# Two attentions: one softmax head at a time and outputs turned at the end, or four heads together and outputs that come out turned

## The chip, the cores and the metric

One core of one Trainium2 chip runs the whole kernel. The metric is the device time of one execution in microseconds; the figure given for a kernel is the median of several runs. The kernel before takes 1696.51 us (median of 3 runs, 1694.89 to 1697.32).

Engines in this text: PE (TensorE) multiplies matrices and also turns (transposes) tiles, DVE (VectorE), ACT (ScalarE) and POOL (GpSimd) work elementwise, SP issues most of the DMAs. Each engine works through its own instructions in order and waits on semaphores for the others.

## The reference, cut to what matters

A decoder trunk of two layers over 512 tokens of width 1024, float32. Each layer adds an attention mixer and then a mixture of experts (MoE) to `x`.

```
even layer: h = rms_norm(x); x += concat(mamba2(h), dsa(h)) @ even_w_out
   dsa: 8 heads of 64, one K and V shared by all heads; for each query the
        128 best earlier keys by an indexer score (selm masks out the others)
        p = softmax(q k^T / 8 + rel_bias);  out = p v
odd layer:  h = rms_norm(x); x += nsa(h) @ odd_w_out
   nsa: 8 heads of 128 in 2 groups of 4; each group has its own K and V for
        three branches: compressed blocks (31 keys), selected blocks, window
        out = g0 * softmax_c(..) v_c + g1 * softmax_s(..) v_s + g2 * softmax_w(..) v_w
each layer: x += MoE(rms_norm(x))    32 experts of 6 MB of weights, top 2 for each token
```

At 512 tokens the selected and the window branch both see all earlier keys, so their scores are as wide as the causal part of the row.

## The kernel before, in words

The layers run one after another: even mixer, MoE, odd mixer, MoE. The part that the change touches are the two softmax attentions, which share one class, `Attention` (line 348), and the head of the output projection that follows each of them, `outproj_pe` (545).

**Work of one attention.** Queries are cut into four tiles of 128 rows, taken from the last tile (i = 3, 512 visible keys) to the first (i = 0, 128 keys); `TILES` is (3, 2, 1, 0). The unit is one head and one branch of one tile, with L = 128 (i + 1) keys, or 31 in the compressed branch. The even attention has 32 units (8 heads, four tiles), the odd one 96 (8 heads, three branches, four tiles; per head: compressed, selected, window). A unit goes through:

1. scores, PE (411): q as stationary, keys as moving, into one of four score banks; in the even layer two heads go as a pair, each on 64 rows of the array, and for i > 0 a second matmul (417) adds the mask.
2. DVE (502): bias is added, the row minimum of the negated scores is taken, the result goes to `p` in SBUF (semaphore `lg`).
3. ACT (489): exp, with the row sum as a by-product (`ex`).
4. PE (428): p is turned in blocks of 128 keys into one of two banks (`tr`).
5. ACT or DVE (476): the turned p is copied to `pT` in SBUF (`copied_act`, `copied_dve`).
6. PE (446), the value products: pT stationary (128 keys by 128 queries), V moving (64 or 128 columns), one matmul for each block of 128 keys (`pv`). The output lies with queries on partitions. It is not normalized yet.

Per head (even: per pair of heads) POOL raises the sums to the power -1 and, in the odd layer, multiplies them by the gates (1314; 1655, 1657, 1659; `coef`). DVE then scales the output and, in the odd layer, adds the three branches (1318; 1663 to 1665; `o`). When four heads of a tile are finished, their scaled outputs are turned on PE (435) and copied to `mixT`, the stationary operand of the output projection (558). In the even layer the Mamba half of the rows is turned in the same way; it is ready before the attention starts.

**Order.** Everything is written out by hand in steps t. At step t PE does the scores of unit t, turns unit t-2 and multiplies unit t-3 by its values; DVE and ACT have matching loops. `p` has 4 slots, `pT` 2.

**After the attention.** `outproj_pe` waits for the DVE's part of the last unit, projects the first half of tile 3, turns what is left (`tail_turns`), and projects on. SP waits for the last `o` (`att.done`, 1956) and then issues the weights of the first two experts; those of the third wait until the projection has been added (`_add`, 1959).

Of the kernel before, what the change touches and what calls it, by code (L numbers as in the profile page):

```python
# [196 lines left out]
def build(nc, ins, out):  # L197
    ctx = ExitStack()
    with ctx:
# [24 lines left out]
        minus1 = sb("minus1", [P, 3])  # L224
# [123 lines left out]
        class Attention:  # L348
            def __init__(self, tag, order, branches, turns, work, weigh, finish, before=None):
                self.weigh, self.finish, self.order = weigh, finish, order  # L350
                self.NB = len(branches(*order[0]))

                self.seq, self.tail = list(turns.get(-1, [])), turns["tail"]
                for m, (i, j) in enumerate(order):
                    for b, br in enumerate(branches(i, j)):
                        self.seq.append(dict(br, m=m, b=b, i=i, j=j))
                    self.seq += turns.get(m, [])
                self.all = self.seq + self.tail

                self.base = dict.fromkeys(("a", "n", "act", "dve", "m"), 0) if before is None else before.after  # L360
                c = dict(self.base)
                for u in self.all:
                    u["n"] = c["n"]; c["n"] += 1
                    if "m" in u:
                        u["a"] = c["a"]; c["a"] += 1
                    c[u["copy"]] += 1
                    u["copied"] = c[u["copy"]]
                c["m"] += len(order)
                self.after = c
                self.by_n = {u["n"]: u for u in self.all}  # L370
                self.by_a = {u["a"]: u for u in self.all if "m" in u}
                self.p = at(work, 4, SEQ)
                self.pT = at(work + 4 * SEQ, 2, 4, P)
                self.negm = sb(f"{tag}_negm", [P, 4])
                self.sums = sb(f"{tag}_sums", [P, 4, self.NB])
                self.coef = sb(f"{tag}_coef", [P, 4, self.NB])
# [4 lines left out]
            def tiles(self, u):  # L381
                return [(kt, min(P, u["L"] - kt * P)) for kt in range((u["L"] + P - 1) // P)]

            def copied(self, eng, u):

                eng.wait_ge(self.sem(f"copied_{u['copy']}"), u["copied"])

            def finished(self, eng, m):

                if m >= 0:  # L390
                    eng.wait_ge(self.sem("o"), self.base["m"] + m + 1)
# [6 lines left out]
            def done(self, eng):  # L398
                self.finished(eng, len(self.order) - 1)

            def mixed(self, eng, i):

                for u in self.all:
                    if "src" in u and u["tile"] == i:
                        self.copied(eng, u)

            def scores(self, pe, us):

                for u in us:
                    self.scored(pe, u["a"] - 4)  # L410
                    mm = nc.tensor.matmul(score_bank[u["a"] % 4][:, 0:u["L"]], u["q"], u["k"],  # L411
# [3 lines left out]
                for u in us:  # L415
                    if "mask" in u:
                        nc.tensor.matmul(score_bank[u["a"] % 4][:, 0:u["L"]], identb[:], u["mask"],
                                         start=False, stop=True).then_inc(self.sem("qk"), 1)

            def turn(self, pe, u):  # L420

                if u["n"] - 2 in self.by_n:
                    self.copied(pe, self.by_n[u["n"] - 2])
                b = bank[2 + u["n"] % 2]
                if "m" in u:
                    pe.wait_ge(self.sem("ex"), u["a"] + 1)
                    for kt, w in self.tiles(u):
# [1895 lines left out]
```

## Time and profile before

| | |
|---|---|
| median of 3 runs | 1696.51 us |
| profiled execution | 1696.19 us, span 1694.4 us |
| even attention | 203.1 to 253.9 us of the span |
| odd attention | 1000.8 to 1122.3 us |
| PE busy over the span | 94% |

The profile is of one execution. Times in its rows are from the start of the span. In a row of the timeline the columns are start, length, engine, line, operation, what it writes and reads, shape, count. A matmul of 32-bit data shows as two instructions (two passes). The lengths of PE's rows contain a modelled tail that overlaps the next instruction, so what an instruction costs PE is read from start to start.

### The profile page before, as it was taken

To read this page: it belongs to the slowest core of one execution; us is meant where nothing else is said; L and a number is where in the kernel's file an instruction comes from. 1 tells how busy PE (TensorE), PEld (TensorE's weight loads), DVE (VectorE), ACT (ScalarE), POOL (GpSimd) and SP (SyncE) were. 2 spreads that over 40 slices of the span, in tenths; PEclk is the share of its full clock that TensorE was granted. 3 is DMA by queue.
4 is the path that set the end of the run, shared out by engine and by line. 5 is a ranking of instruction groups with operands and counts; after the bars stand their busy time and mean duration, and the time that the engine had idled before them with its cause. 6 is when DMAs were issued, how large, how long until landed. Compare 5 with 4: busy or idle time off the path is not lost.

```text
span 1694.4 us, 20980 instructions
## 1 busy us (share of the span) xinstructions
PE 1589.3 (94%) x7948; PEld 753.0 (44%) x7948; DVE 434.3 (26%) x1112; ACT 393.7 (23%) x897; POOL 200.4 (12%) x297
## 2 busy tenths in 40 slices
PE   7999899799999999998799989999799999999993
PEld 4545574433333333332446457855333333333331
DVE  1585651610000000000321235643500000000002
ACT  2444451311111111111100136632211111111110
POOL 1241220000000000000101012320000000000000
PEclk9999999899999999999899989999799999999997
DMA  7120307379999999999924120042699999999996
GB/s 236 64 86 7 112 5 297 137 300 421 421 422 421 422 421 423 422 422 371 302 34 170 39 66 2 1 184 115 250 413 422 421 421 422 422 422 422 423 422 248
DMA packets 117162, 467.24 MB, mean 276 GB/s; under 512 B 40346, under 2 KB 46746, under 8 KB 68205
## 3 DMA queue, kind: packets, MB, share of 16 engines
q1 hardware_dynamic: 107724, 449.63, 66.1%
q10 hardware_dynamic: 4256, 8.40, 1.4%
q0 software_dynamic: 5120, 8.41, 1.3%
q8 instruction: 36, 0.59, 0.1%
q14 instruction: 26, 0.21, 0.0%
HBM read 455.88 MB, written 18.91 MB: 280 GB/s over the span
## 4 chain that ended last, share of the span: by engine, by line
PE 77%; SPq 11%; DMA 5%; DVE 3%; issue 2%; ACT 1%; POOL 1%; ACTq 0%; DVEq 0%; POOLq 0%
PE bank L1793 19%; PE bank L1806 10%; SPq L1741 9%; PE bank L1768 9%; PE bank L1432 8%; PE bank L558 7%; PE bank L811 6%; PE bank L446 4%; DMA arena<-in_moe_w_up 3%; PE bank L411 3%; PE bank L1783 2%; SPq L1750 2%; PE bank L892 2%; PE bank L428 2%; PE bank L1799 1%
## 5 line engine op out<-in xcount | busy, mean ns | idle before, releaser
L1793 PE MATMUL bank<-arena 128*64 128x512 f32 x2048 | 451.4, 592 | 8.1 <-DMA arena<-in_moe_w_up 6.7
L1793 PEld LDWEIGHTS bank<-arena 128*64 128x64 f32 x2048 | 143.5, 137 | 304.6 <-issue 294.0
L1806 PE MATMUL bank<-arena 128*64 128x512 f32 x1024 | 230.6, 592 | 2.2 <-DVE arena L1897 2.2
L1893 DVE TENSOR_TENSOR arena<-arena,bank 128x256 f32<-128x256 f32 x64 | 26.9, 421 | 644.4 <-ACT arena L1883 644.4
L1768 PE MATMUL bank<-arena 128*64 128x512 bf16 x1280 | 168.2, 395 | 9.7 <-DVE arena L1763 6.4
L1812 POOL DMA_INDIRECT y_d<-arena,slot_row x64 | 62.7, 979 | 904.7 <-ACT arena L1888 891.1
L1432 PE MATMUL bank<-arena 128*128 128x512 f32 x320 | 138.1, 593 | 0.8 <-ACT arena L328 0.8
L1806 PEld LDWEIGHTS bank<-arena 128*64 128x64 f32 x1024 | 72.2, 137 | 124.5 <-issue 111.2
L1883 ACT ACTIVATE arena<-bank 128x256 f32<-128x256 f32 x64 | 24.5, 383 | 408.2 <-PE bank L1793 408.2
L558 PE MATMUL bank<-arena 128*128 128x512 f32 x256 | 111.9, 594 | 0.0
L811 PE MATMUL bank<-arena 128*128 128x512 f32 (+1 forms) x288 | 105.3, 525 | 0.0
L1768 PEld LDWEIGHTS bank<-arena 128*64 128x64 bf16 x1280 | 69.4, 113 | 68.5 <-issue 10.4
L1432 PEld LDWEIGHTS bank<-arena 128*128 128x128 f32 x320 | 60.6, 190 | 77.1 <-issue 76.1
L446 PE MATMUL bank<-arena 128*128 128x128 f32 (+1 forms) x544 | 83.3, 278 | 4.0 <-DVE arena L476 2.9
L1888 ACT ACTIVATE arena<-bank 128x512 f32<-128x512 f32 x64 | 38.2, 597 | 190.0 <-PE bank L1806 190.0
L1779 ACT ACTIVATE gain<-bank 128x512 f32<-128x512 f32 x64 | 38.2, 597 | 180.7 <-PE bank L1768 180.7
L446 PEld LDWEIGHTS bank<-arena 128*128 128x128 f32 x544 | 70.8, 191 | 13.0 <-DVE arena L476 6.2
L811 PEld LDWEIGHTS bank<-arena 128*128 128x128 f32 x288 | 49.8, 190 | 54.5 <-issue 54.5
L558 PEld LDWEIGHTS bank<-arena 128*128 128x128 f32 x256 | 47.9, 190 | 56.4 <-issue 56.4
L411 PE MATMUL bank<-arena 128*128 128x31 f32 (+8 forms) x256 | 70.6, 415 | 1.6 <-ACT arena L1557 0.9
L502 DVE CUSTOM_DVE_ANT_0 arena<-bank,arena 128x512 f32<-128x512 f32 (+3 forms) x128 | 52.4, 415 | 67.9 <-PE bank L411 47.6
L1897 DVE COPY arena<-bank 128x256 f32<-128x256 f32 x64 | 27.1, 424 | 133.0 <-PE bank L1799 133.0
(287 smaller groups left out, 1434.8 us busy)
## 6 DMA issues: line engine op xcount, KB each, us to landing
arena<-in_moe_w_gate SPq DMA_DIRECT2D x128, 1024.0 KB, 20.1
arena<-in_moe_w_up SPq DMA_DIRECT2D x128, 1024.0 KB, 22.9
arena<-in_moe_w_down SPq DMA_DIRECT2D x62, 2048.0 KB, 23.2
arena<-in_even_w_in SPq DMA_DIRECT2D x4, 2048.0 KB, 7.9
arena<-y_d ACTq DMA_DIRECT2D x8, 1024.0 KB, 8.2
arena<-bias_row_d SPq DMA_DIRECT2D x2, 3584.0 KB, 11.6
arena<-in_odd_w_in SPq DMA_DIRECT2D x3, 2048.0 KB, 8.9
arena<-in_even_w_out SPq DMA_DIRECT2D x2, 2048.0 KB, 8.0
```

The lines of the kernel that those rows point to most:

```text
L411: mm = nc.tensor.matmul(score_bank[u["a"] % 4][:, 0:u["L"]], u["q"], u["k"], start=True, stop="mask" not in u)
L446: mm = nc.tensor.matmul(bank[4 + u["m"] % 2][:, u["b"] * D:(u["b"] + 1) * D], self.pT[0:w, u["a"] % 2, kt, :], u["v"](kt), start=(kt == 0) ...
L502: ins_ = nc.vector.tensor_tensor_reduce(out=self.p[:, u["a"] % 4, 0:L], in0=score_bank[u["a"] % 4][:, 0:L], in1=u["bias"], scale=-1.0, sca ...
L558: mm = nc.tensor.matmul(mix_bank(n)[:, :], mixT[:, k, i * P:(i + 1) * P], wo[half][:, k, :], start=(k == 0), stop=(k == KD - 1))
L811: mm = nc.tensor.matmul(o, l, r, start=(k == 0), stop=(k == KD - 1))
L1432: mm = nc.tensor.matmul(o, lhs(k), rhs(k), start=(k == 0), stop=(k == KD - 1))
L1741: sp.dma_start(wgu[u][:, n, 4 * h:4 * h + 4].rearrange("p (e j) f -> p e (j f)", e=1), src).then_inc(S(f"{t}_{('wgu', 'wgv')[h]}{u}"), 16)
L1768: mm = nc.tensor.matmul(bank[4][h * CAP:(h + 1) * CAP, :], pick[:, i, :], parts[part][i][:, h * 512:(h + 1) * 512], start=(part == 0 and i ...
L1779: return nc.scalar.activation(xe, bank[4][:, :], ACT.Copy)
L1793: mm = nc.tensor.matmul(bank[1][fh * CAP:(fh + 1) * CAP, :], xeT[:, j, half * CAP:(half + 1) * CAP], wgu[u][:, :, n, fh * FH:(fh + 1) * FH ...
L1806: mm = nc.tensor.matmul(bank[3][dh * CAP:(dh + 1) * CAP, :], hidT[:, j, fh * CAP:(fh + 1) * CAP], wd[u][:, n, dh * 512:(dh + 1) * 512], st ...
L1812: return nc.gpsimd.indirect_dma_start(out=y_d[layer][:, :], out_offset=bass.IndirectOffsetOnAxis(ap=slot_row[:, n:n + 1], axis=0), in_=yb[ ...
```

## The change

The outputs come out of the value products already turned. Four heads that share V form a quad: in the even layer four heads of one tile; in the odd layer the four heads of a group in one branch, in the order selected, window, compressed. V is now the stationary operand, and the turned p of the four heads (512 columns) moves past it. In the even layer V has 64 columns, so two products, each with two heads (256 columns), go to the two halves of the output partitions. In the odd layer all three branches of a group accumulate in one PSUM bank. Since the output has queries along its columns, it can't be scaled by row any more; so p itself is multiplied by its coefficient (gate over sum) on DVE before it is turned. The DVE instructions that scaled and added outputs are gone, as are the turns of the outputs; ACT copies the finished bank to `mixT`.

The steps become: for a quad whose last unit is at step `last`, DVE scales at `last + 2` (and `last + 3` where 4 L is over 1024), PE turns at up to `last + 6`, value products follow from `last + 7`, one block of keys a step. `p` has 8 slots. Turned blocks of several heads share a bank where L is short. The output projection of tile 3 is pulled in ahead of the last quad's turn.

```diff
+            TURN, SCALE = 6, 2
...
+                for n, q in enumerate(quads):
+                    L, last = q["L"], 4 * n + 3
+                    q["m"], q["nk"] = c["m"], (L + P - 1) // P
...
+                    per = 4 if 4 * L <= DM else 2
+                    for k in range(4 // per):
...
+                        self.scale_at[last + self.SCALE + k].append(dict(quad=q, lo=per * k, n=per))
+                    per, q["groups"] = NT // q["nk"], []
+                    for lo in range(0, 4, per):
...
+                        self.turn_at[4 * n + lo + per - 1 + self.TURN].append(g)
+                    for kt in range(q["nk"]):
+                        self.value_at[last + self.TURN + 1 + kt].append((q, kt))
+                    if q["last"]:
+                        self.out_at[last + self.TURN + 1 + q["nk"]].append(q)
...
+                for g in self.groups:
+                    g["n"], g["copy"] = c["n"], ("act", "dve")[c["n"] % 2]
...
+                self.p = at(work, 8, SEQ)
             def turn(self, pe, g):
+                if g["n"] - 2 in self.by_n:
+                    self.copied(pe, self.by_n[g["n"] - 2])
...
+                    pe.wait_ge(self.sem("sc"), us[-1]["scaled"])
+                    for kt in range(q["nk"]):
+                        for r, u in enumerate(us):
+                            c = (kt * len(us) + r) * P
+                            mm = nc.tensor.transpose(b[0:w, c:c + P], self.p[:, u["a"] % 8, kt * P:kt * P + w], ident[:])
...
+            def values(self, pe, q, kt):
+                if kt == 0:
+                    for g in q["groups"]:
+                        self.copied(pe, g)
+                    if q["first"]:
+                        self.out(pe, q["o"] - 2)
+                for o, v, pT in q["products"](bank[4 + q["o"] % 2], self.pT[q["m"] % 2][:, kt], kt):
+                    mm = nc.tensor.matmul(o, v, pT, start=(q["fresh"] and kt == 0), stop=(q["ends"] and kt == q["nk"] - 1))
...
+            def pe(self, pe, drain):
+                for t in range(self.steps):
+                    if t < len(self.units):
+                        u = self.units[t]
+                        if not (u.get("paired") and u["r"] % 2):
+                            self.scores(pe, [u, self.units[t + 1]] if u.get("paired") else [u])
+                    if t == len(self.units) + NT:
+                        drain()
+                    for g in self.turn_at[t]:
+                        self.turn(pe, g)
+                    for q, kt in self.value_at[t]:
+                        self.values(pe, q, kt)
...
             def dve(self, dve, link):
+                for t in range(self.steps):
+                    if t < len(self.units):
                         dve.wait_ge(self.sem("qk"), u["a"] + 1)
+                        if t >= 8:
+                            dve.wait_ge(self.sem("tr"), self.units[t - 8]["group"]["n"] + 1)
                         ins_ = nc.vector.tensor_tensor_reduce(...).then_inc(self.sem("lg"), 1)
+                    for op in self.scale_at[t]:
+                        dve.wait_ge(self.sem("coef"), q["m"] + 1)
+                        nc.vector.tensor_tensor(p, p, att_coef[...].broadcast_to((P, n, q["L"])), ALU.mult).then_inc(self.sem("sc"), 1)
+                    for g in self.turn_at[t]:
+                        if g["copy"] == "dve":
+                            self.copy_out(dve, g)
             def act(self, act):
+                for t in range(self.steps):
+                    for g in self.turn_at[t]:
+                        if g["copy"] == "act":
+                            self.copy_out(act, g)
+                    for q in self.out_at[t]:
+                        act.wait_ge(self.sem("pv"), q["m"] + 1)
+                        nc.scalar.activation(q["dst"], split(bank[4 + q["o"] % 2][:, :], 4, P), ACT.Copy).then_inc(self.sem("o"), 1)
+                    if t < len(self.units):
...
...
-            project(0, TILES[0])
-            att.tail_turns(pe)
-            for i in TILES[1:]:
+            def drain():
+                att.scored(pe, att.after["a"] - 1)
+                project(0, TILES[0])
+            att.pe(pe, drain)
+            project(0, TILES[1])
+            att.done(pe)
+            for i in TILES[2:]:
                 project(0, i)
...
-        def even_finish(a, dve, link, u):
-        def odd_finish(a, dve, link, u):
+            def products(o, pT, kt):
+                return [(o[r * HD:(r + 1) * HD, half * 2 * P:(half + 1) * 2 * P], kvd[:, kt, O_V:O_V + HD], pT[:, r::2, :])
+                        for r in range(2)]
+            def products(o, pT, kt):
+                v = vc[:, g, :] if b == CMP else vv[:, b - 1, kt, g * OD:(g + 1) * OD]
+                return [(o[:, :], v, pT)]
+        odd_att = Attention([odd_quad(i, g, b) for i in TILES for g in range(OG) for b in (SEL, WIN, CMP)], ...)
```

The first of the two `products` is the even layer's, the second the odd layer's. `even_finish` was one DVE instruction for each pair of heads, `odd_finish` three for each head.

POOL's work (`even_weigh`, `odd_weigh`) is the same, once for each quad on four numbers a row, in place of once for each pair on two (even) or each head on three (odd).

## Rows read from the trace of the kernel before

**Rows 1.** The page: busy time of the engines over the span.
```profile
PE 1589.3 (94%) x7948; PEld 753.0 (44%) x7948; DVE 434.3 (26%) x1112; ACT 393.7 (23%) x897; POOL 200.4 (12%) x297
```

**Rows 2.** Windows: the even attention, then the odd one by query tile.
```profile
core 0: us, PE busy (x) PEld busy (x) DVE busy (x) ACT busy (x) POOL busy (x), PEclk, DMA share, GB/s
203.10:253.90 50.80, 49.82 (x356) 37.01 (x357) 27.04 (x99) 27.49 (x83) 11.44 (x17) 0.97 0.22 56
1000.50:1041.50 41.00, 40.39 (x250) 30.10 (x251) 20.22 (x76) 23.50 (x64) 9.12 (x21) 0.94 0.04 3
1041.50:1074.80 33.30, 32.81 (x232) 26.88 (x231) 20.40 (x81) 21.03 (x66) 10.40 (x24) 1.00 0.00 1
1074.80:1100.40 25.60, 24.78 (x184) 21.71 (x183) 17.79 (x82) 17.47 (x67) 10.40 (x24) 1.00 0.01 2
1100.40:1122.30 21.90, 18.25 (x138) 15.90 (x137) 17.00 (x90) 15.10 (x68) 11.35 (x26) 1.00 0.01 2
```

**Rows 3.** Windows of the output projection after the even attention.
```profile
254.00:290.00 36.00, 36.00 (x94) 16.59 (x94) 3.90 (x7) 3.70 (x10) 0.23 (x1) 1.00 0.85 350
290.00:318.00 28.00, 28.00 (x119) 16.57 (x117) 14.02 (x15) 10.11 (x16) 3.98 (x9) 1.00 0.00 1
```

**Rows 4.** Timeline of PE, odd attention, one head at 512 keys.
```profile
1011.16 1.02 PE L411 MATMUL bank<-arena 128*128 128x512 f32 x2
1012.02 0.60 PE L428 MATMUL bank<-ident,arena 128*128 128x128 f32 x4
1012.46 1.06 PE L446 MATMUL bank<-arena 128*128 128x128 f32 x8
1013.35 1.02 PE L411 MATMUL bank<-arena 128*128 128x512 f32 x2
...
1015.22 0.31 PE L411 MATMUL bank<-arena 128*128 128x31 f32 x2
1015.36 0.64 PE L428 MATMUL bank<-ident,arena 128*128 128x128 f32 x4
```

**Rows 5.** Timeline of PE, even attention, one pair of heads at 512 keys.
```profile
211.38 1.13 PE L411 MATMUL bank<-arena 64*128 64x512 f32 x4
...
212.88 0.60 PE L428 MATMUL bank<-ident,arena 128*128 128x128 f32 x4
213.32 1.00 PE L446 MATMUL bank<-arena 128*128 128x64 f32 x8
214.16 0.60 PE L435 MATMUL bank<-ident,arena 128*128 128x128 f32 x4
```

**Rows 6.** Timeline of PE: products on 64 columns in pairs, between products on 128.
```profile
32.72 1.45 PE L811 MATMUL bank<-arena 128*128 128x512 f32 x3
34.10 7.09 PE L837 MATMUL bank<-arena 128*64 128x512 f32 x32
41.12 2.06 PE L811 MATMUL bank<-arena 128*128 128x140 f32 x15
```

**Rows 7.** Timeline, odd attention: from one score of 512 keys to its head's coefficients.
```profile
1009.52 0.69 DVE L502 CUSTOM_DVE_ANT_0 arena<-bank,arena 128x512 f32<-128x512 f32 x1 [1.49 <-PE bank L411]
1010.26 0.72 ACT L489 ACTIVATE arena<-arena,oa_negm 128x512 f32<-128x512 f32 x1 [1.19 <-DVE oa_negm L502]
1011.16 0.23 POOL L1655 TENSOR_SCALAR oa_coef<-oa_sums 128x3 f32<-128x3 f32 x1 [2.96 <-ACT arena L489]
1012.43 0.19 POOL L1659 TENSOR_TENSOR oa_coef<-oa_coef,gates 128x3 f32<-128x3 f32 x1
```

**Rows 8.** Groups by form: odd attention, tile 0 (DVE, ACT), then POOL's power.
```profile
L502 DVE CUSTOM_DVE_ANT_0 arena<-bank,arena 128x128 f32<-128x128 f32 x16 | 4.4, 285 | 2.2 <-PE bank L411 2.1
L489 ACT ACTIVATE arena<-arena,oa_negm 128x128 f32<-128x128 f32 x16 | 6.4, 399 | 4.6 <-DVE oa_negm L502 4.5
...
L1657 POOL TENSOR_TENSOR oa_coef<-oa_coef,minus 128x3 f32<-128x3 f32 x32 | 28.1, 879 | 2.7
L1170 POOL TENSOR_TENSOR ssq<-ssq,nhalf 128x4 f32<-128x4 f32 x1 | 1.1, 1051 | 0.1
```

**Rows 9.** Timeline of DVE: a multiply-class instruction on 1024 elements from SBUF.
```profile
298.18 1.21 DVE L671 TENSOR_TENSOR arena<-arena 128x1024 f32<-128x1024 f32 x1
```

More of the change, by code:

```diff
@@ L378, in sem, with copied @@
             def sem(self, what):
                 return S(f"att_{what}")
[L381 to L391, printed above, removed]
+            def copied(self, eng, g):
+                eng.wait_ge(self.sem(f"copied_{g['copy']}"), g["copied"])
@@ L398, in done @@
             def done(self, eng):
-                self.finished(eng, len(self.order) - 1)
+                self.out(eng, self.after["o"] - 1)
             def mixed(self, eng, i):
-                for u in self.all:
-                    if "src" in u and u["tile"] == i:
-                        self.copied(eng, u)
+                for g in self.groups:
+                    if g.get("tile") == i:
+                        self.copied(eng, g)
+                self.out(eng, max(q["o"] for q in self.quads if q["tile"] == i))
             def scores(self, pe, us):
@@ L450, in pe @@
-            def pe(self, pe):
-                N = len(self.seq)
-                for t in range(N + 3):
-                    u = self.seq[t] if t < N else {}
-                    if "m" in u and not (u.get("paired") and u["b"] % 2):
-                        self.scores(pe, [u, self.seq[t + 1]] if u.get("paired") else [u])
-                    if 2 <= t < N + 2:
-                        self.turn(pe, self.seq[t - 2])
-                    if t >= 3 and "m" in self.seq[t - 3]:
-                        self.values(pe, self.seq[t - 3])
@@ L479, in act @@
             def act(self, act):
-                for t in range(len(self.all) + 2):
-                    if t >= 2 and self.all[t - 2]["copy"] == "act":
-                        self.copy_out(act, self.all[t - 2])
-                    if t < len(self.seq) and "m" in self.seq[t]:
-                        u = self.seq[t]
-                        p = self.p[:, u["a"] % 4, 0:u["L"]]
+                for t in range(self.steps):
[6 more added lines that the diff above has]
+                    if t < len(self.units):
+                        u = self.units[t]
+                        q, slot = u["quad"], u["a"] % 8
+                        p = self.p[:, slot, 0:q["L"]]
@@ new lines, in products, with even_turn @@
+            def products(o, pT, kt):
+                return [(o[r * HD:(r + 1) * HD, half * 2 * P:(half + 1) * 2 * P], kvd[:, kt, O_V:O_V + HD], pT[:, r::2, :])
+                        for r in range(2)]
+            return dict(tile=i, L=L, units=units, products=products, first=half == 0, fresh=True, ends=True, last=half == 1,
+                        dst=mixT[:, 4:8, i * P:(i + 1) * P])
+        def even_turn(i):
+            return dict(tile=i, src=rows_m[:, 0, i, :], dst=mixT[:, 0:4, i * P:(i + 1) * P], ready=(S("ssm_row"), NT))
@@ L1350, in build @@
+        even_att = Attention([even_quad(i, half) for i in TILES for half in range(2)],
+                             {1 + i: even_turn(i) for i in range(NT)}, 2 * EW + 2 * KD * 512, O_XBCS, even_weigh)
         o0 = HEADS * TW
@@ L1677, in build @@
[L1677 to L1686 removed]
+            pool.wait_ge(S("recip"), 2 * n + 2)
@@ L1689, in build @@
+        odd_att = Attention([odd_quad(i, g, b) for i in TILES for g in range(OG) for b in (SEL, WIN, CMP)],
+                            {}, O_OW + 2 * KD * 512, O_CT, odd_weigh, before=even_att)
         weight = sb("weight", [P, 2, NT])
```

248 lines of the change are left out of this document (102 added, 146 removed).

## The prediction, written before the changed kernel was run

> **What bounds the kernel now.** The page comes first: PE is busy 94% of the span, the next engine 26% [rows 1]. Then windows over the two stages that the change touches: 50.8 us for the even attention and 121.5 us (1000.8 to 1122.3) for the odd one, 41, 33, 26 and 22 us by query tile [rows 2]. PE is busy over 96% of each but the last, where it is at 83%. So the question is how much PE work the change takes out, and whether PE is still fed in time.
>
> Behind an attention the output projection keeps PE busy without a hole, while the first experts' weights load in 254 to 290 us and the DMA queues then stand still to 318 us [rows 3]. A shift of the attention's end moves everything behind it by the same amount. The weights are now issued only after the last output copy, some 10 us later against PE (7 us of projection, then turn, copy, product, copy); the 28 us of idle DMA cover that, so it costs nothing. Without this cover it would be up to 10 us for each layer.
>
> **PE's work, part by part.** Start to start, at 512 keys: one head's scores .86 us, a turned block .11 (four .44), four value products .89, compressed scores .14 [rows 4]. One value product is thus .22 for 128 moving columns, and four are .89; its successor with V stationary moves 512 columns, as the scores do, for .86. Turning operands round saves next to nothing in the odd layer, since the same columns pass. What goes there: 8 turns of outputs at .44, 3.5 us, and about 1.4 in the products. By these pieces the odd attention held about 107 us of PE work and now holds 102 (by tile 38, 30, 21 and 12.5; narrower tiles scaled by columns), each plus 2 us for the slow clock at its start (clock .94 in tile 3, the 1.2 GHz level for part of it, [rows 2]). The other 12.5 of the 121.5 us are waits.
>
> In the even layer V has only 64 columns. Before, eight passes of 64 columns took .84 [rows 5], the same as 128 columns would: .21 a product, 80 of them, 16.8 us. Now a pair of products runs on two column halves. Such pairs stand elsewhere in the trace: 32 instructions of 512 columns in 7.02 us, .44 for two at once [rows 6], so a pair of passes over 256 columns is .21 and the two passes .43. But the row ahead shows that going into this mode costs extra: three instructions of 128 columns take 1.38 in place of 1.28, and the pairs 7.02 in place of 6.86. That is about .26 for in and out, and each quad's block stands alone between turns and scores. I take .70 for each of 20 blocks, 14.0 us; the ends are .43 (no switching cost, 8.6) and .86 (no overlap, 17.2). Four turns of outputs at .44 go too. Net: -2.8 - 1.8 = -4.6 us.
>
> The Trainium skill ("TensorEngine Tiling (Array Packing)", Key Properties) says that changing the tiling mode drains the engine, while tiles of one mode run in parallel. By its second half alone the even gain would be 10 us; by the first it shrinks. The trace agrees with both, at about .1 us for each change of mode.
>
> **The other engines.** At 512 keys a quad costs DVE four reductions at about .61 start to start, two scalings of two heads (1024 elements, 1.21 us, [rows 9]), and two copies at .6: 6 us beside 8.7 of PE (odd) or 7.4 (even). The three scaling instructions for each odd head go. ACT loses copies and gains 12 output copies of .6. Neither becomes the bound by its sum.
>
> **The wait that is added.** A turn now waits for the scaling, that for the coefficient, and that for the quad's last exp. Priced at 512 keys: score end to DVE start .2, reduction to exp start .74, exp to POOL's start .90 [rows 7], POOL 1.47 for three numbers [rows 7] plus .17 for a fourth (.88 for three, 1.05 for four, [rows 8]), a hop .1, scaling 1.2, a hop .1: 4.9 us. In the even layer POOL does the power alone, and it is 4.3. Queued behind DVE's wait are the next reductions and copies, and behind those ACT's exps and PE's turns.
>
> What lies on PE between a quad's last score and its first turn (`last + 3`)? From selected to window: value products and wide scores, 5.7 us at 512 keys. Enough. From window to compressed: one turn (.44), two steps of .14 + .44, and .14, since value products of the quad before start only at `last + 3`: 1.74 us. PE stands for 3.2 us. This falls on 2 of 6 quads a tile: 6.5 us in tile 3. In tile 2 the chain is 4.4 and the cover 1.4: 6 us. A second wait: DVE may write a p slot only when the unit eight before is turned, and a compressed quad is turned all at once at its `last + 6`; so the window's first reduction waits for PE one step ahead, DVE then has two reductions and a scaling to do, and PE's next turn stands about 1 us (tile 3) to 1.5 (tile 2), 3.5 in all.
>
> In the short tiles DVE's own circle decides, for it stands in the scaling's wait. At 128 keys: reduction .33 and exp .5 [rows 8], POOL and hops 1.8, scaling .6, half a copy .3, one more reduction .2: 3.7 us a quad, 3.3 behind a compressed one, 10.9 for three against 6.2 of PE work. At 256 keys 13.3 against 10.6. So waits of 9.4 us in tile 0, less 3 for the last chain, which the projection covers, and 5.4 in tile 1. Add 2.3 us at the start (first turn after seven scores) and .7 at the end.
>
> Sum odd: 102 + 2 + 2.3 + 6.5 + 6 + 3.5 + 5.4 + 6.4 + .7 = 135 against 121.5: **+13.5 us**, with 31 us of waits where 12.5 were.
>
> Sum even: all quads are alike, so at 512 and 384 keys about 7.5 and 5.8 us of PE work cover the 4.9 to the first turn (4.3 and a second reduction, since two scores end together). Waits: 1.5 at the start, 1 in tile 1 (circle 4.4 against 4.0), 1 in tile 0, .7 at the end, about 4, as many as now (50.8 less 45.2 of pieces less 1.5 of slow clock). **-5 us**.
>
> Total 1696.2 (profiled: 1694.4 span and 1.8 around it) + 8.5 = 1704.7; that execution lies .3 below the median, which leaves 1704 to 1705. I predict 1704. Ends: even between -10 and -2; each of the eight window-to-compressed waits and the DVE circle at half or at the full price plus a copy (.6) in the way: odd between +2 and +17.
>
> **Rivals.**
> A. The scaled weights arrive in time, and the odd layer is bound by PE's sum. It would need a chain of 1.7 us in place of 4.9, or PE behind its own schedule so that the scores lie longer ahead of the turns. For it: PE never stood for POOL before, though there nobody but DVE waited for it. Against: the score and the turn are both PE's, so PE can't be late for one and not for the other. Odd then 102 + 2 + 5 = 109, -12.5; even -5: 1679 us. It decides from where the window-to-compressed wait is under about 1 us.
> B. The waits come about half as long, since they swallow waits that were there anyway: odd +5, even -5, 1696 us.
> C. More than priced: the column halves don't overlap in this short form (even -2), or a PE that stands a third of the time drops to its slower clock. In tile 0 PE was busy 83% at clock 1.00 [rows 2]; now it would be near 60%. A tile 0 at the lower level would cost another 6 us or so: 1711 us.
>
> **Chances.** Forecast .58, A .10, B .17, C .15. No change within .2% (3.4 us, what a measurement of this kernel can tell) holds most of B and a bit of the forecast; faster holds A and a part of B. Faster .17, same .15, slower .68. The range takes in C and B's centre and leaves A out: 1692 to 1711.
>
> **What would show it.** Idle time of PE ahead of the turns, ended by DVE's scaling, in the odd attention: about 3 us at each change from window to compressed in tiles 3 and 2. POOL as what DVE waits for longest. PE busy in tile 0 at 60 to 70%. Even attention's end near 249 us. Value products in the even layer at .6 to .75 for each block. If PE's waits for DVE in the odd attention sum to under 15 us, the forecast is wrong; if the odd stage takes over 130 us, it is right.

## The result, and the profile after

The changed kernel takes 1745.8 us (median of 4 runs, 1737.6 to 1749.6) against 1696.9: 1.028 times the kernel before (95% interval 1.024 to 1.033), 49 us slower. 1704 had been predicted, and 1711 was the upper end. The profiled execution took 1742.2, span 1740.1.

The page after, first line; it answers to [rows 1]. PE is busy for 7 us more than before, although 416 of its instructions went.
```profile
PE 1596.2 (92%) x7532; PEld 721.5 (41%) x7532; DVE 441.8 (25%) x1027; ACT 385.5 (22%) x860; POOL 190.4 (11%) x265
```
Windows of the same stretches as [rows 2], same columns: even attention, then odd tiles 3, 2, 1, 0.
```profile
206.00:254.40 48.40, 43.49 (x256) 21.77 (x256) 32.81 (x88) 27.33 (x81) 8.70 (x9) 0.93 0.22 58
1002.90:1052.00 49.10, 40.71 (x130) 22.88 (x131) 26.27 (x64) 20.25 (x57) 7.75 (x17) 0.81 0.02 2
1052.00:1094.20 42.20, 33.71 (x140) 19.65 (x139) 21.93 (x67) 18.56 (x59) 8.41 (x17) 1.00 0.00 1
1094.20:1132.90 38.70, 28.46 (x115) 18.19 (x114) 16.46 (x60) 15.44 (x57) 10.19 (x21) 0.88 0.00 0
1132.90:1166.60 33.70, 22.23 (x93) 15.39 (x92) 11.92 (x65) 13.80 (x54) 8.78 (x19) 0.83 0.00 1
```
The profiled spans differ by 45.7 us: 42.1 in the odd attention (121.5 to 163.7), 1.9 in the projection behind it, 3.0 ahead of the even attention, -.8 from the even attention's first score to its projection's last product. The rest agrees within .5. The 3.0 don't come from the change: a stretch at the low clock at 21 us stands in the traces of the changed kernel, e2 and e9 below, whose even attention starts at 206.0 to 206.3 us, and in none of the others, where it starts at 202.1 to 203.5.

Two things are new in the odd rows. PE is idle for a sixth to a third of each tile, and the clock column is .81, .88 and .83 in tiles 3, 1 and 0. TensorE's clock has two levels, 1.2 and 2.4 GHz, so .81 over 49.1 us means that 2 x .19 of it, 18.7 us, were spent at 1.2 GHz. Over the stage that is 39 us, in which PE was busy for 36; at 2.4 GHz that work takes 18.

So the trace splits the 163.7 us into 107.1 of busy time at 2.4 GHz, 18.0 for the low level, and 38.5 in which PE stands. (Before: 114.0, 2.2 and 5.3.) Each of the 22 stands over .3 us begins behind a modelled tail of about .16 us, which counts as busy. Taking the 102 of work that were predicted, 18 and 43.7 of waits remain. The waits of the odd attention, by what ended them (us in total, times, longest):
```profile
DVE arena L529 <- PE bank L433: 51.6, 43, 5.2
...
DVE arena L529 <- PE bank L454: 18.8, 9, 3.3
PE bank L454 <- DVE arena L541: 16.8, 9, 3.5
DVE arena L541 <- POOL att_coef L1678: 14.5, 11, 2.7
...
PE bank L469 <- DVE arena L498: 10.6, 6, 3.0
...
PE bank L469 <- ACT arena L498: 5.7, 6, 1.6
PE bank L469 <- issue: 5.2, 2, 4.3
```
L433 is a score, L529 the reduction behind it, L454 a turn, L469 a value product, L541 the scaling, L498 the copy of a turned block. The first of PE's rows was foretold (turns wait for the scaling). That value products wait for *copies* was not. The longest wait of the "issue" row, 4.3 us in tile 1, is one of them too: VectorE's copy at 1111.13 stood behind a scaling at 1109.99, which had waited 2.74 us for GpSimd. The two kinds lie in different places: of PE's stands over .3 us, 16.2 us in tiles 3 and 2 are ahead of turns and .4 ahead of value products; in tiles 1 and 0 it is .7 and 20.8.

### The profile page after: what moved, and what is told of

Its sections match the earlier page's. It is cut to its first block, busy times and chain, and to the rows that moved or that the text cites. A ratio compares the mean times of both kernels' runs of the same rounds, so it can differ in the third digit from the quotient of the medians.

```text
span 1740.1 us, 19760 instructions
## 1 busy us (share of the span) xinstructions
PE 1596.2 (92%) x7532; PEld 721.5 (41%) x7532; DVE 441.8 (25%) x1027; ACT 385.5 (22%) x860; POOL 190.4 (11%) x265
## 4 chain that ended last, share of the span: by engine, by line
PE 75%; SPq 11%; DMA 5%; DVE 4%; issue 2%; ACT 2%; POOL 2%; ACTq 0%; DVEq 0%; POOLq 0%
PE bank L1806 19%; PE bank L1819 9%; SPq L1754 9%; PE bank L1781 8%; PE bank L1452 8%; PE bank L583 6%; PE bank L841 6%; PE bank L469 4%; DMA arena<-in_moe_w_up 3%; PE bank L433 2%; PE bank L1796 2%; PE bank L454 2%; SPq L1763 2%; PE bank L922 2%; PE bank L1812 1%
## 5 line engine op out<-in xcount | busy, mean ns | idle before, releaser
L1819 PEld LDWEIGHTS bank<-arena 128*64 128x64 f32 x1024 | 71.9, 137 | 124.4 <-issue 111.1
L841 PE MATMUL bank<-arena 128*128 128x512 f32 (+1 forms) x288 | 106.9, 531 | 0.0
L1781 PEld LDWEIGHTS bank<-arena 128*64 128x64 bf16 x1280 | 69.4, 113 | 68.7 <-issue 10.6
L469 PE MATMUL bank<-arena 128*128 128x512 f32 (+1 forms) x176 | 72.0, 569 | 26.1 <-DVE arena L498 12.8
L1452 PEld LDWEIGHTS bank<-arena 128*128 128x128 f32 x320 | 60.6, 190 | 77.1 <-issue 76.1
L516 ACT ACTIVATE arena<-arena,att_negm 128x512 f32<-128x512 f32 (+4 forms) x128 | 63.5, 497 | 77.7 <-DVE att_negm L529 70.0
L433 PE MATMUL bank<-arena 128*128 128x31 f32 (+8 forms) x256 | 72.3, 435 | 1.6 <-ACT arena L1576 0.9
L841 PEld LDWEIGHTS bank<-arena 128*128 128x128 f32 x288 | 50.5, 192 | 55.5 <-issue 55.5
L529 DVE CUSTOM_DVE_ANT_0 arena<-bank,arena 128x512 f32<-128x512 f32 (+4 forms) x128 | 51.4, 415 | 83.6 <-PE bank L433 56.5
L583 PEld LDWEIGHTS bank<-arena 128*128 128x128 f32 x256 | 48.0, 190 | 58.2 <-issue 58.2
L454 PE MATMUL bank<-ident,arena 128*128 128x128 f32 (+1 forms) x272 | 48.5, 304 | 18.9 <-DVE arena L541 18.6
```

The source lines that it names most:

```text
L433: mm = nc.tensor.matmul(score_bank[u["a"] % 4][:, 0:u["quad"]["L"]], u["q"], u["k"], start=True, stop="mask" not in u)
L454: mm = nc.tensor.transpose(b[0:w, c:c + P], self.p[:, u["a"] % 8, kt * P:kt * P + w], ident[:])
L469: mm = nc.tensor.matmul(o, v, pT, start=(q["fresh"] and kt == 0), stop=(q["ends"] and kt == q["nk"] - 1))
L516: nc.scalar.activation(p, p, ACT.Exp, bias=att_negm[:, slot:slot + 1], scale=-1.0, accum_out=att_sums[:, q["m"] % 4, u["r"]:u["r"] + 1]).t ...
L583: mm = nc.tensor.matmul(mix_bank(n)[:, :], mixT[:, k, i * P:(i + 1) * P], wo[half][:, k, :], start=(k == 0), stop=(k == KD - 1))
L841: mm = nc.tensor.matmul(o, l, r, start=(k == 0), stop=(k == KD - 1))
```

## Experiments

Each is compared with the kernel before on the same chip. A difference to the changed kernel is one of medians, 1745.8 us and the run's. "Stage" is the odd attention from its first score to the first projection product (before 121.5, after 163.7), "low" the part of PE's busy time in it at 1.2 GHz, halved: what the low level cost (before 2.2, after 18.0). "Standing" is the time in the stage in which PE is idle (before 5.3, after 38.5).

**e1: the even attention changed, the odd one as before.** (The old class is used for the odd layer.)

> The even attention as changed, the odd attention as it was before. Theory: the loss of 49 us is all in the odd attention, and the even one by itself gives what its own work gives: its columns save 4.6 us, its waits take back up to 4, so 1691 to 1696 us, and the odd stage is again 121 us long at clock 1.00 behind its first 5 us. Rival 1 (the step of the prediction): 1691. Rival 2: the even part is itself a loss (column halves that don't overlap, slower clock): over 1698.

1697.2 us, ratio 1.000 (.999 to 1.001). Stage 121.4 at clock .98. The whole loss is in the odd attention, and the even part by itself changes nothing that can be measured; the gain that the theory gave it (1691 to 1696) is not there. Its value products are cheap. In the changed kernel's trace one block of keys of a quad (four instructions) takes .58 us start to start and the four turns beside it .59, 1.17 together, where 1.14 was priced:
```profile
222.91 0.65 PE L469 MATMUL bank<-arena 128*64 128x256 f32 x4
223.50 0.66 PE L454 MATMUL bank<-ident,arena 128*128 128x128 f32 x4
224.09 0.65 PE L469 MATMUL bank<-arena 128*64 128x256 f32 x4
```

**e2: the copies of a step ahead of its scaling, on VectorE.**

```diff
-                    for op in self.scale_at[t]: ...   # wait coef, scale
                     for g in self.turn_at[t]:
                         if g["copy"] == "dve":
                             self.copy_out(dve, g)
+                    for op in self.scale_at[t]: ...
```


> VectorE's copy of a step now stands ahead of the scaling of the same step; nothing else is changed. Theory A (the value products of one quad wait because VectorE's copy is queued behind the next quad's scaling, and that waits for the coefficient): the 10.7 us that TensorE's value products wait for VectorE's copies go, the circle in tiles 1 and 0 gets shorter, part of the low clock goes with it: 1728 to 1738 us. Theory B (the circle is the chain from the last exp to the scaling alone, and the copy only happens to end it): the same wait moves to the next turn, 1743 to 1748 us.

1727.2 us, ratio 1.018 (1.016 to 1.020): 18.6 us less for two loops exchanged. The profiled executions differ by 14.2, of which 11.4 lie in the stage, now 152.3: low 12.8 (5.2 less), standing 32.7 (5.8 less). Tile 1 takes 33.7 us (38.7 in the changed kernel), tile 0 27.0 (33.7), tiles 3 and 2 within 1 us of the changed kernel's. PE's waits for VectorE's copies fell from 10.6 to 5.2 us, while its turns wait 19.7 for 16.8. Theory A holds, though the time is .8 us below its range; why is best seen in the changed kernel itself, one quad of tile 0 (timeline of all engines; the rows in between are left out):
```profile
1137.62 0.23 POOL L1674 TENSOR_SCALAR att_coef<-att_sums 128x4 f32<-128x4 f32 x1 [4.65 <-ACT arena L516]
...
1137.81 0.60 PE L454 MATMUL bank<-ident,arena 128*31 128x128 f32 x4
1137.93 1.04 POOL L1676 TENSOR_TENSOR att_coef<-att_coef,minus 128x4 f32<-128x4 f32 x1
...
1139.29 0.69 DVE L541 TENSOR_TENSOR arena<-arena,att_coef 128x512 f32<-128x512 f32 x1 [0.21 <-POOL att_coef L1678]
...
1139.89 0.67 DVE L498 COPY arena<-bank 31x512 f32<-31x512 f32 x1
...
1140.62 1.73 PE L469 MATMUL bank<-arena 128*128 128x512 f32 x2 [1.98 <-DVE arena L498]
...
1142.14 1.33 PE L433 MATMUL bank<-arena 128*128 128x128 f32 x6
```
By its start-to-start time (.44 us) the turn was done at 1138.3 and its copy could start. It stands behind the *next* quad's scaling (1139.29), and that behind GpSimd. The value product waits for the copy, and the next scores (1142.14), with the last ones of a quad among them, wait behind the value product, since PE works in order. Those scores then feed the next coefficient. So the copy and the value product are links of the circle. In every second round it closes another way: the value product at 1146.19 was released by a copy on ScalarE, which stood behind an exp whose reduction (1144.52) had waited for a turn to free its p slot.

**e5: the changed kernel without GpSimd's power** (line 1676 and its wait). The coefficient is then no reciprocal: this part of the computation is left out, and nothing else.

> The changed kernel without GpSimd's power in the odd attention: the coefficient is the clamped sum times the gate and not its reciprocal, so this part of the computation is left out. It takes about 1.1 us out of the chain from the last exp to the scaling (1.04 for the power and a hop). Theory (the circle in tiles 1 and 0 and the window-to-compressed waits in tiles 3 and 2 run through this chain): 12 quads, 4 transitions and the first fill get 1.1 us shorter each, 19 us, and some low clock goes with it: 1718 to 1729 us. Rival (other waits take over at once, copies or p slots): 1735 to 1746 us.

1725.4 us, 1.017 (1.016 to 1.019); stage 146.6, low 9.2, standing 30.1. The time is the theory's, 20 us less, and the chain is in the circle. The split is not the theory's: it gave 19 us to the waits and some low clock on top. The stage is 17.1 us shorter, 8.4 by less standing and 8.8 by the clock. Ahead of turns the waits fell by 5.4 us (16.8 to 11.4), ahead of value products by 3.3 (21.5 to 18.2), so less than half of the 19 us was won as waiting, and the clock made up the number.

**e6: twelve p slots for eight.** A reduction waits for the turn of the unit twelve before.

> The changed kernel with twelve p slots in the odd attention, turns and scalings where they were. It takes away only the wait of a reduction for the turn of the unit eight before. The prediction priced that wait at 3.5 us (tiles 3 and 2). Theory: it is worth that, 3 to 5 us, and something in tile 0, where an exp and the copy behind it wait for such a reduction: 1738 to 1743 us. Rival (the slots are what makes the circle): below 1725 us. Rival (VectorE would have waited for scores anyway): 1744 to 1748 us.

1736.1 us, 1.023 (1.021 to 1.024); stage 157.6, low 17.3, standing 33.8. 9.7 us less, over the theory's 3 to 5 and 2 us below its range, and far from the first rival. In the stage it is 6.1 us, of which .7 is clock: 5.4 where 3.5 had been priced (4.7 by the standing).

**e12: copies first, and the odd coefficients on VectorE, eight slots.**

```diff
+                        if self.weigh is None and lo == 0:
+                            dve.wait_ge(self.sem("ex"), q["units"][-1]["a"] + 1)
+                            c_ = att_coef[:, q["m"] % 4, :]
+                            link(nc.vector.scalar_tensor_tensor(c_, att_sums[:, q["m"] % 4, :], 1e-30,
+                                 gl[:, q["tile"], q["b"], 4 * q["g"]:4 * q["g"] + 4], ALU.max, ALU.mult))
+                            nc.vector.reciprocal(c_, c_).then_inc(self.sem("coef"), 1)
```


> The changed kernel with only two edits: copies ahead of scalings, and the odd coefficients on VectorE; eight slots, turns and scalings at the old steps. The two edits gave 18.6 us (copies first) and 20.4 us (power left out) when made alone or nearly so. Theory (both act on the same circle, so they add only in part, the wide tiles' transitions take only the chain's part): 1706 to 1714 us. Rival (they are separate terms and add, with the low clock that goes with them): 1700 to 1706 us.

1712.2 us, 1.010 (1.007 to 1.013); stage 138.9, low 3.7. The time is in the theory's range: 33.6 us less, where e2 and e5 would add to 39.0, though this edit takes more out of the chain than e5's. The two edits act on one circle and add only in part. Tiles 3 and 2 still take 41.8 and 42.1 us (33.1 and 32.1 in e10 below): there the lead is too short, whatever the order.

**e3: a longer lead.** Twelve slots, and in the odd attention turns nine steps behind, scaling five. O_ROWS is where the third block of four p slots lies.

```diff
-            TURN, SCALE = 6, 2
+            ... TURN=9, SCALE=5, more=O_ROWS
-                        if t >= 8: ... self.units[t - 8] ...
+                        if t >= self.slots: ... self.units[t - self.slots] ...
```


> Odd attention with twelve p slots in place of eight, turns nine steps behind the first score of a quad's group in place of six, scaling five steps behind the last score in place of two. Theory (all of the loss is lack of lead: latency between the last score and the first turn, and the low clock that follows from the standing TensorE): TensorE's waits in the odd stage fall from 44 to about 10 us, the low clock after the first 5 us goes, the odd stage takes 110 to 118 us: 1692 to 1700 us. Rival (a circle through VectorE or ScalarE bounds the short tiles however long the lead is): tiles 3 and 2 get back to 40 and 31 us, tiles 1 and 0 stay above 30 us each: 1715 to 1725 us.

1706.3 us, 1.007 (1.004 to 1.009); stage 126.3, low 1.7. The number lies between both. The low clock behind the first 5 us is gone, as the theory says, but PE still stands for 19.4 us, where about 10 were expected.

**e7: e3 with copies first; e8: e7 with the value products one step later** (`value_at[last + TURN + 2 + kt]`, both layers).

> The kernel with the long lead (twelve slots, turns nine steps behind, scaling five), which took 1706 us, with VectorE's copies ahead of its scaling in each step. There 7.1 us of the value products' waits were ended by VectorE's copies. Theory: a copy behind a scaling is what ends them; 4 to 7 us less, 1699 to 1702 us. Rival (a value product stands one short step behind its turn, and the copy of .6 to .7 us itself doesn't fit in): 1704 to 1707 us.

> As the kernel with the long lead and the copies ahead of the scaling, and the value products of a quad one step later, in both layers. Theory (what is left in tiles 1 and 0 is the copy between turn and value product): the 12 us that value products wait there fall to under 4: 1692 to 1698 us. Rival (ScalarE's exps or VectorE bound the short tiles): 1699 to 1704 us.

1702.0 us (1.004, 1.002 to 1.005) and 1700.3 (1.002, 1.001 to 1.003). e7 is at the upper edge of what was expected. In e8 the time is the rival's, but not its reason. PE's waits in the odd stage, e7, then e8 (L460 turns, L475 value products):
```profile
PE bank L460 <- DVE arena L549: 8.9, 9, 1.7
PE bank L475 <- DVE arena L504: 4.3, 6, 1.1
PE bank L475 <- ACT arena L504: 3.2, 5, 0.9
```
```profile
PE bank L460 <- DVE arena L549: 12.3, 13, 1.7
PE bank L475 <- DVE arena L504: 2.3, 3, 0.8
PE bank L475 <- ACT arena L504: 1.3, 3, 0.5
```
The waits for copies halve, and those for the scaling (L549) grow by nearly as much: five steps is too late, because the scaling then stands behind reductions whose scores PE issues just ahead of the turn.

**e9, e10, e11: the scaling four steps behind, three, and three with VectorE's coefficients.**

> As the kernel with the long lead, copies first and value products one step later (1700.3 us; its TensorE still stands 14 us for the scaling at turns), but the scaling four steps behind a quad's last score in place of five. Theory (there the scaling is placed too late in VectorE's order: it stands behind a reduction that waits for a score one step ahead of the turn): 6 to 10 of the 14 us go, odd stage 113 to 117 us, 1691 to 1695 us. Rival (four steps are too few for the chain in tile 0, and VectorE stands before the coefficient): what is won in tiles 3 and 2 is lost in tiles 1 and 0, 1699 to 1703 us.

> The same with the scaling three steps behind the last score. The theory has its optimum where the wait for the coefficient (chain 4.9 us at 512 keys, 3.1 at 128) equals what lies on TensorE in those steps: at 128 keys three steps are 1.6 us. I expect it to win in tile 3 and lose in tile 0 against four steps: 1692 to 1697 us. Rival: earlier is always better, under 1690 us.

> The same with three steps, and the odd layer's coefficients worked out on VectorE (clamp times one plus exp of minus the gate's logit, then a reciprocal, about .15 us each) ahead of the scaling, in place of three instructions on GpSimd (1.5 us and hops). Theory: 1.2 us less of chain lets three steps be enough in the short tiles: 3 to 6 us below the same kernel with GpSimd's coefficients, 1686 to 1691 us. Rival (VectorE's extra two instructions and its standing at the last exp cost as much): no gain.

1689.4 us (.9955, .9939 to .9970), 1688.2 (.9954, .9941 to .9967) and 1688.0 (.9954, .9943 to .9965). All three beat the kernel before, by 7 to 9 us. Stages 111.3, 111.1 and 111.1. Four steps did what the theory said, with a time 2 us below its range. Three did not lose in tile 0 (22.1 us in both), so my optimum was wrong; that earlier is better is not shown either, since the two times agree within their spread. VectorE's coefficients, two instructions of .15 and .18 us, gave nothing more, as the rival had it: with enough lead the chain's length is covered. The windows of e10, tiles 3 to 0:
```profile
998.30:1031.40 33.10, 30.75 (x114) 16.82 (x115) 22.93 (x59) 18.82 (x53) 7.93 (x15) 0.94 0.05 3
1031.40:1063.50 32.10, 32.10 (x143) 19.73 (x142) 22.91 (x70) 18.99 (x60) 9.59 (x18) 1.00 0.00 1
1063.50:1087.30 23.80, 23.79 (x118) 16.44 (x116) 16.82 (x62) 15.49 (x56) 9.34 (x18) 1.00 0.00 1
1087.30:1109.40 22.10, 18.07 (x101) 12.57 (x101) 13.22 (x69) 13.95 (x57) 9.82 (x20) 1.00 0.01 2
```
PE is busy for 104.7 us, 2.0 of it the low level's, and stands for 6.4. The stage is 10.4 us shorter than before, but not all of that is won: the turns and value products of two quads now stand between products of the projection, which takes 70.9 us from its first product's start to its last one's, for 66.8 before. From the first score to the projection's last product it is 182.0 for 188.3: once PE is fed, the operands turned round are worth 6.3 us in the odd layer.

**e4, e13, e14: work that nobody needs, in PE's waits.** Extra products of the identity with itself, into the bank that the next turn overwrites.

```diff
+                    if "b" in q and q["tile"] > 1 and g["lo"] == 0 and (q["b"] == WIN or q is self.quads[0]):
+                        for _ in range(8):
+                            nc.tensor.matmul(b[:, 0:P], ident[:], ident[:], start=True, stop=True)
                     pe.wait_ge(self.sem("sc"), us[-1]["scaled"])
...
+                    if "b" in q and q["tile"] < 2:
+                        n = q["groups"][-1]["n"]
+                        self.copied(pe, self.by_n[n - 1])
+                        for _ in range(4):
+                            nc.tensor.matmul(bank[2 + (n + 1) % 2][:, 0:P], ident[:], ident[:], start=True, stop=True)
```
(e14; e13 has CMP for WIN; e4 has four at every quad's first turn in tiles 1 and 0, none in tiles 3 and 2.)

> In tiles 1 and 0 of the odd attention TensorE runs four extra 128-column products (.44 us at the full clock, results never read) ahead of the wait for the scaling at a quad's first turn, and four more ahead of the wait for the copies at its value products: 12 quads x .88 = 10.6 us of work, most of it in time in which TensorE stands. Theory (the low clock is a cost of its own, some 9 us in these two tiles, and comes from TensorE standing): the low stretches of tiles 1 and 0 go, the granted clock there is 1.00, and the time is 1736 to 1745 us although work was added. Rival (the clock falls whatever TensorE does there, or what it costs lies in the waits): clock unchanged, 1746 to 1756 us.

> The changed kernel with extra 128-column products, results never read, only where its trace shows TensorE standing: eight (.88 us) ahead of the first turn of the first quad and of the four compressed quads of tiles 3 and 2 (their waits are 1.7 to 3.5 us), four (.44 us) ahead of the value products in tiles 1 and 0 (.5 to 4.3 us). That is 9.7 us of work in time that was idle. Theory (the low clock is a term of its own and comes from standing; the last filler test put half of its work where nothing stood): busy time at the low level in the odd stage falls from 36 us to under 20, which is 8 us or more of time, and the kernel takes 1730 to 1739 us. Rival (a lower clock only fills time in which TensorE would wait anyway, so its removal gives nothing): the clock rises, the waits grow, and the time stays 1742 to 1748 us.

> The last filler kernel (1743.3 us) had its products in tiles 3 and 2 ahead of the compressed quads' first turns, while the 1.7 to 3.5 us of standing there are ahead of the window quads' first turns. Here they stand at the window quads; everything else is the same. Theory (the low clock is a cost of its own): 3.5 us of added work moves from a busy place into idle time, and TensorE's busy time at the low level falls further below 21 us: 1733 to 1739 us. Rival (the clock only fills waits): the 3.5 us that no longer stand in the way are all that is won, 1739 to 1741 us, and the waits grow by what the clock gives.

All three expectations priced the extra work at half of what it takes. A turn is one instruction for each block, .11 us; such a product of 32-bit numbers is two, so eight products take 1.8 us and four .9. Two rows of e14, the sixteen instructions of one eight and the turn behind them:
```profile
1038.42 2.05 PE L452 MATMUL bank<-ident 128*128 128x128 f32 x16
1041.87 0.66 PE L457 MATMUL bank<-ident,arena 128*128 128x128 f32 x4 [1.40 <-DVE arena L549]
```
The work added is thus some 21 us in e4 and 19.5 in e13 and e14.

e4: 1747.1 us (1.031, 1.028 to 1.034), stage 166.9, low 13.0, standing 27.3. e13: 1743.3 (1.028, 1.027 to 1.030), stage 165.5, low 10.4, standing 29.0. e14: 1730.7 (1.021, 1.019 to 1.022), stage 152.3, low 3.9, standing 21.0. The first two missed the theory's range and lie in the rival's, although the low clock fell in both. They leave it open: half of e4's extra work, and the eights of e13 but one, stood where PE did not wait. e14 settles it. With 19.5 us of useless products, nearly all of them in front of waits (behind three of the fours no wait is left), the changed kernel is 15 us *faster*; by the rival it could at best be as fast. It is also 12.6 us faster than e13, from which it differs only by the place of four eights: 7.1 us of work, which is the most that the rival leaves to be won. Its windows:
```profile
1000.70:1044.70 44.00, 40.49 (x179) 24.61 (x180) 25.84 (x64) 19.89 (x56) 7.35 (x15) 0.95 0.03 2
1044.70:1086.70 42.00, 37.58 (x172) 23.24 (x171) 21.92 (x67) 18.81 (x61) 8.79 (x18) 1.00 0.00 1
1086.70:1124.00 37.30, 30.21 (x148) 21.15 (x147) 16.54 (x60) 15.42 (x56) 9.24 (x20) 0.95 0.00 0
1124.00:1153.00 29.00, 22.96 (x150) 17.99 (x149) 11.95 (x65) 13.36 (x54) 9.58 (x19) 1.00 0.00 1
```
Against the changed kernel the low level's share fell by 14.1 us and the stage by 11.4. The added work and the standing that is left come to 2.7 us more than the standing before: most of what the low level costs is time of its own. The Trainium skill ("TensorE: Matmul & The Clock Gate", "HAM oscillation — how this bites in real kernels") prices it as half of the time at the low level: by its rule an estimate of 19.5 us for the 39 here, where I take half of PE's busy time in it, 18. e14 took away 31.2 us at the low level, 15.6 by that rule and 14.1 by mine, and 11.4 us of time went: the size agrees, and no run here tells the two apart.

## Why the prediction was wrong

The sign was right, and so was the mechanism in tiles 3 and 2, where turns wait for the scaling. Two steps failed: the term for the slower clock (2 us for 18), and the circle of the short tiles, which was set up without the value product's wait for its copy (11.8 us of waits in tiles 1 and 0, where PE stands for 21.5). Nothing in the range covered both. In the profiled execution, 37.5 us above the 1704.7 of the sum, the stage has 28.7 of the miss, the even attention with its projection 4.2, the projection behind the odd one 1.9, and 3.0 lie ahead of everything that was changed; the median lies 3.6 above that execution.

*Right, or nearly.* PE's odd work at 2.4 GHz, 102 us: e10's stage holds 104.7 - 2.0 = 102.7, and 2.8 more of the attention's turns and products stand inside its projection, by .44 and .96 each. The work before was priced too low, 107 us for a busy time of 114.0: the 12.5 us called waits contradict [rows 2], whose odd windows leave PE idle for 5.6. So the change takes out more work than the 5 us that the prediction saw. The even value block with its turns, 1.17 us for 1.14. GpSimd's power on four numbers, 1.04 for 1.05. The later issue of the experts' weights, nothing. The first turn's wait, 2.1 for 2.3. The turns at the change from window to compressed, 3.5 in tile 3 and 3.2 in tile 2 for 3.2 and 3.0 (the other two were 1.7 and 2.4). Here is the larger one; the turn it stops is the window quad's first:
```profile
1042.29 0.66 PE L454 MATMUL bank<-ident,arena 128*128 128x128 f32 x4
1042.79 0.31 PE L433 MATMUL bank<-arena 128*128 128x31 f32 x2
1046.54 1.08 PE L454 MATMUL bank<-ident,arena 128*128 128x128 f32 x4 [3.45 <-DVE arena L541]
```

*Wrong, 16 us: the clock.* The sum had 2 us for the low level; it cost 18.0. Rival C named it, but for tile 0 alone, at 6 us (measured 5.6), and left out tile 3 (8.6, of which 2.5 at its start) and tile 1 (3.7). I judged by PE's busy share of a whole tile. The rows show the clock falling in tile 3 too, where PE was busy for 83% of the time, behind a stretch with 4.67 us busy of 6.80 and no stand over 2.13. Stretches of the changed kernel's trace, alternately at 2.4 and 1.2 GHz:
```profile
1007.90:1014.70 6.80, 4.67 (x14) 2.02 (x13) 4.99 (x12) 3.87 (x11) 1.49 (x3) 1.00 0.00 0
1014.70:1018.10 3.40, 3.40 (x15) 2.76 (x14) 2.29 (x7) 2.17 (x6) 0.58 (x2) 0.50 0.00 0
...
1144.40:1151.20 6.80, 2.81 (x17) 2.04 (x17) 3.61 (x21) 2.90 (x13) 2.34 (x5) 1.00 0.01 2
1151.20:1154.70 3.50, 3.50 (x12) 2.30 (x13) 0.30 (x2) 0.99 (x4) 0.30 (x2) 0.51 0.00 0
```
The low stretches are the fully busy ones: PE stands, the clock falls, and the work that then comes takes twice as long.

*Wrong, 13 us: "In the short tiles DVE's own circle decides ... 3.7 us a quad".* The circle takes 5.3 us in tile 0 (value products start at 1140.6, 1146.2, 1151.0, 1156.4 and 1161.8; the rounds without a low stretch, the second and the fourth but for its last .3 us, took 4.9 and 5.3). I had put only the engines ahead of the scaling into it, with half a copy, and took for granted that PE's scores lie ahead. They don't: they are queued behind a value product, which waits for a copy, which is queued behind a scaling. By my estimate from start-to-start times, the rest of the copy (.3), the value product (.86) and the last scores (.4) are the missing 1.6 us. e2 shows that the copy's place is in the circle, e5 that the chain is; the sizes of the single links were not tested. (The circle's three quads were also summed to 10.9 us, where 3.7, 3.7 and 3.3 make 10.7.) Waits were 43.7 us in place of 31, or 38.5 as the trace counts them, and the p slots had 2 of these: 5.4 for 3.5.

*Even, 3 of 5 us.* At equal clock the even attention with its projection takes 113.9 us (e7) against 116.0: -2.1 for the -5 forecast. I allowed 4 us of waits, "as many as now", but the kernel before has none there: its PE stands nowhere over .3 us within the stage, and what I took for waits was work that my pieces missed. The changed kernel's PE does stand, 4.7 us in five places and .8 behind the projection's start. In e1 low stretches of the clock, 5.6 us for 1.7, take the rest back.

Of the marks set down beforehand, waits ended by the scaling, value blocks (just under the .6 given) and "odd over 130" came as said. GpSimd is not what DVE waits for longest: 14.5 us, behind 51.6 for scores and 18.8 for turns. The even end came at 254.4, or 251.4 less the 3.0 from before it, for 249. PE's busy share of tile 0 was 66%, within the 60 to 70% given. They told the mechanism, not its size.

What stays open: what starts a low stretch was not isolated. The even attention has one that begins at 244 to 249 us in seven of the eight traces whose even part is the changed kernel's (all but e3's), and in none of the seven with the copies first (e2, e7 to e12), so the order seems to matter there too, and a part of what e2 won outside the stage may lie there. Nor is it known why the changed kernel's runs lie 12 us apart (1737.6 at a mean clock of .967, 1749.6 at .960) where e14's five lie within 1.8.

## What to carry to other kernels

When a change puts a new wait on an in-order engine, follow the circle through every queue until it comes back to where it began; a copy or a product behind the waiting instruction belongs to it, and the order of two loops was worth 18.6 us here, part of it through the clock. A bottleneck engine that starts to stand pays twice, for the wait and for the work behind it at the lower clock, so add both to the sum. And a scheme that loses for lack of lead can win with the same instructions: here a longer lead, the copies first, value products a step later and the scaling's place took it from 1745.8 to 1688.

## What was not expected of the hardware

Useless products, .9 and 1.8 us at a time and 19.5 us in all, ahead of waits made a kernel faster by 15 us (e14), through the clock. And the runs of kernels spread very differently, which nothing here explains: 12 us in the changed kernel's four, 2.1 in e10's seven and 1.8 in e14's five, but also 8.5 in ten of e9 and 10.5 in 22 of the kernel before, whose PE hardly stands.
